# Retention's rotation moved from TensorE and ScalarE to VectorE, and a second token group multiplied before the norm's root

## The chip, the cores and the metric

The program runs on one core of one Trainium2 chip. The metric is the device time of one execution in microseconds. The engines are TensorE (PE, with its weight loads PEld), VectorE (DVE), ScalarE (ACT), GpSimd (POOL) and SyncE (SP), which issues the DMAs here.

## What is computed

Two blocks of two layers each act on a stream x of 512 tokens by 1024 channels in float32. The change lies in the first block only:

```
for l in range(2):
    h = rms_norm(x, norm_g[l])
    (gu, gv, gz, rq, rk, rv, rz, dq, dk, dv, dz, a_f, b_f, a_b, b_b) = split(h @ w_in[l])
    y_a = gmlp_branch(gu, gv, gz, ...)      # gelu(u) * mix(layer_norm(gelu(v))) * silu(z)
    y_b = retention_branch(rq, rk, rv, rz, ...)
    y_c = gdn_branch(dq, dk, dv, dz, ...)
    x = x + sum_n(sigmoid(h @ w_gate_n) * (y_n @ w_branch_out_n)) @ w_out[l]
x = rms_norm(x, final_norm_g)

def rotary(x):                              # on rq and rk, per head of 128
    x1, x2 = x[..., :64], x[..., 64:]
    return concatenate([x1 * cos - x2 * sin, x2 * cos + x1 * sin])

# retention, per head: o = (q k^T / sqrt(128) * mask) v, then a group norm;
mask = exp(where(rel >= 0, lf * rel, -lb * rel))      # lf, lb = log_sigmoid(decay_logit)
```

The second block is an attention with a SwiGLU, twice, and is the same in both kernels.

## The kernel before

**Data.** x is held as eight tiles of 128 channels by 512 tokens (`xT[:, k]`). Every projection is made to float32 precision from rounded halves: a weight granule of 512 KB comes by DMA into `raw[g % 4]` (`hi` waits for it), ACT casts it to `wh` (`hi(g)`, 128x1024), POOL writes `wl = raw - wh` in two pieces of 128x512 (`split`, L2361), and then PE does three matmuls for every 128-deep step: `wh*hh`, `wl*hh` and `wh*hl` (`three`, L830 to L832), where `hh` and `hl` are the rounded activations and their rest. There are four slots of each, and a slot's next load waits until its `wl` is written. A granule serves one `feature_tile` (eight steps, 24 matmuls of 128x512, one bank, a result with channels on the partitions) or a quarter of a `token_tiles` group (two steps for each of four banks, a result with tokens on the partitions).

**Order by hand.** Each engine has its own program, tied by semaphores. In a layer of the first block PE goes: token group of granules 0 to 3 (v of the gMLP), the small tile `wab`, feature tiles 4 to 7 (u), token group 8 to 11 (retention's v, `rv`), feature tiles 12 to 19 (retention's q and k), the retention products, feature tiles 20 to 35, and the rest. The four banks 0 to 3 are used in turn; `taken(i)` waits until the bank's last content is read out (`proj_taken`).

**The norm.** The first token group does not wait for the root of the norm: ACT writes `hh = x * g` (`gained_x`, L1702) and the squares (L1705), DVE writes `hl` (L2605) and adds the squares up (`ssum`, L2599), and the root is applied when ACT reads the banks out with Gelu (`vg`, L1775). In between, PE sums the squares per token (`norm_sums`, L840, after bank 1 of granule 1) and spreads the inverse root over a bank (`norm_row`, L847, after granule 1); from then on DVE writes x times the root (`ht`), ACT its `hh` (`normal_hi`) and POOL its `hl` (L2400) over the old ones, tile by tile as granules 0 to 3 are done.

**Retention.** ACT copies each q or k tile from its bank to `qraw` (L1806). PE multiplies `qraw` by a 128x128 matrix that swaps the halves with a sign (`rotate`, L968, into banks 4 to 7), DVE multiplies that by sin (L2705), `qraw` by cos (L2706) and adds (L2709). `mask_arg` makes the exponent of the mask on 128x896 in three DVE instructions (L2696 to L2698), ACT takes its exponential. `scores(h)` (L987) are four matmuls of 128x512 in float32, DVE multiplies them by the mask (`pb`, L2716), and PE makes the output from sixteen small ones (L998).

Of the kernel before, what the change touches and what calls it, by code (L numbers as in the profile page):

```python
# [16 lines left out]
F32 = mybir.dt.float32  # L17
# [5 lines left out]
P = 128  # L23
# [29 lines left out]
for _name, _n in (("ident", 128), ("ones", 128), ("rot", 128), ("cos", 512), ("sin", 512), ("dist", 896),  # L53
                  ("tri", 256), ("neg", 256), ("level", 2 * LEVELS * 128), ("own", 4), ("turn", 4)):
    CON[_name] = slice(_at, _at + _n)
    _at += _n
# [3 lines left out]
def constants():  # L60
# [5 lines left out]
    rot = np.zeros((P, P), np.float32)  # L66
    rot[i[:64] + 64, i[:64]] = -1.0
    rot[i[:64], i[:64] + 64] = 1.0
    c[:, CON["rot"]] = rot
# [3 lines left out]
    c[:, CON["sin"]] = np.tile(np.sin(ang), (2, 1))  # L73
# [55 lines left out]
def layer_signals(nc):  # L129
# [5 lines left out]
        rot_done=8, rot_taken=8, rope_ready=8,  # L135
        arg_ready=4, mask_ready=4, score_done=16, p_ready=16, o_done=4, o_taken=4,
# [17 lines left out]
DVE_OWN = 78 + 2 * (SUB - 1)  # L154
# [302 lines left out]
def build(nc, stream, params, consts, consts2, gains, xin, memin, out, n_granules):  # L457
# [226 lines left out]
    eye_loaded = nc.alloc_semaphore("eye_loaded")  # L684
    stored = nc.alloc_semaphore("stored")
# [7 lines left out]
    seventh_tile = nc.alloc_semaphore("seventh_tile")  # L693
# [46 lines left out]
    with block:  # L740
        @block.sync
        def _(sp):
# [20 lines left out]
            def projection_loads(a0, from_turn):  # L763

                with sp.Fori(a0 + from_turn, a0 + 5) as a:
# [60 lines left out]
        def _(pe):  # L826
# [23 lines left out]
            with pe.Fori(0, DEPTH) as L:  # L850
# [39 lines left out]
                def norm_sums():  # L890

                    pe.wait_ge(eye_loaded, 16)
# [10 lines left out]
                def token_tiles(g0, between={}):  # L903

                    for j in range(4):
                        weights(g0 + j)
                        for t in range(NT):
                            if j == 0:
                                taken(g0 + t)
                            if j == 0 and g0 == 0:  # L910
                                wait("x_ready", 5 + t)
                            for kk in range(2):
                                k = 2 * j + kk
                                if g0 == 0 and t == 0:
                                    wait("xl_ready", k + 1)
                                w = (g0 + j) % SLOTS
                                cols = slice(kk * T, (kk + 1) * T)
                                m = three(bk[t], hh[:, k, t * P:(t + 1) * P], hl[:, k, t * P:(t + 1) * P],
# [2553 lines left out]
```

## Time and profile before

| | |
|---|---|
| three runs | 2660.8, 2663.35, 2666.52 us (median 2663.35) |
| the profiled execution | 2666.1 us, its span on the core 2664.3 us |
| PE busy | 2590.4 us, 97% of the span |
| DVE, ACT, POOL busy | 39%, 42%, 50% |
| DMA | 215.08 MB, mean 81 GB/s |

The span runs from the first to the last instruction; the 1.8 us around it are in the execution's time only. PE is busy nearly throughout, so two things can change the time: work that PE no longer does, and moments in which it stands still or runs at the lower of its two clocks. The rows below are taken from those moments and from that work.

### The profile page before, as it was taken

To read this page: it belongs to the slowest core of one execution; us is meant where nothing else is said; L and a number is where in the kernel's file an instruction comes from. 1 tells how busy PE (TensorE), PEld (TensorE's weight loads), DVE (VectorE), ACT (ScalarE), POOL (GpSimd) and SP (SyncE) were. 2 spreads that over 40 slices of the span, in tenths; PEclk is the share of its full clock that TensorE was granted. 3 is DMA by queue.
4 is the path that set the end of the run, shared out by engine and by line. 5 is a ranking of instruction groups with operands and counts; after the bars stand their busy time and mean duration, and the time that the engine had idled before them with its cause. 6 is when DMAs were issued, how large, how long until landed. Compare 5 with 4: busy or idle time off the path is not lost.

```text
span 2664.3 us, 37275 instructions
## 1 busy us (share of the span) xinstructions
PE 2590.4 (97%) x13040; PEld 2080.5 (78%) x13040; DVE 1030.9 (39%) x2175; ACT 1117.2 (42%) x1708; POOL 1331.9 (50%) x1024
## 2 busy tenths in 40 slices
PE   7999999999999999999999999999999989999999
PEld 6778888888877788888886558888887756888887
DVE  4565542114466744212557553111005484311100
ACT  5428444325524645333546533333224464333321
POOL 5423664557542465556753114666547302456653
PEclk9999999999999999999999999999999999999999
DMA  4212112333231211332521012322333201233232
GB/s 178 87 46 74 56 33 65 101 95 121 81 94 40 80 33 33 95 94 75 162 82 56 22 32 79 110 94 94 102 111 103 80 16 48 88 101 94 94 103 71
DMA packets 62348, 215.08 MB, mean 81 GB/s; under 512 B 7296, under 2 KB 10496, under 8 KB 61824
## 3 DMA queue, kind: packets, MB, share of 16 engines
q1 hardware_dynamic: 62208, 213.28, 25.4%
q8 instruction: 80, 1.31, 0.2%
q14 instruction: 60, 0.49, 0.1%
HBM read 211.16 MB, written 2.10 MB: 80 GB/s over the span
## 4 chain that ended last, share of the span: by engine, by line
PE 59%; DVE 5%; ACT 1%; issue 1%; POOL 0%; DVEq 0%; ACTq 0%
PE bank L830 15%; PE bank L832 15%; PE bank L831 15%; PE pair L1588 2%; PE pair L830 1%; PE pair L831 1%; PE pair L832 1%; PE bank L1547 1%; PE bank L1548 1%; PE bank L1570 1%; PE pair L1401 1%; DVE soft L3255 1%; DVE pair L2796 0%; PE bank L1203 0%; DVE prod L2795 0%
## 5 line engine op out<-in xcount | busy, mean ns | idle before, releaser
L2361 POOL TENSOR_TENSOR wl<-raw,wh 128x512 fp32r<-128x512 f32 x768 | 1025.0, 1358 | 1174.2 <-ACT wh L1992 381.6
L830 PE MATMUL bank<-hh,wh 128*128 128x512 f32 x1584 | 627.5, 396 | 3.8 <-DVE y L2839 2.3
L832 PE MATMUL bank<-hh,wl 128*128 128x512 f32 x1584 | 617.2, 390 | 0.3 <-issue 0.3
L831 PE MATMUL bank<-hl,wh 128*128 128x512 f32 x1584 | 616.7, 389 | 0.0
L830 PEld LDWEIGHTS bank<-hh,wh 128*128 128x128 f32 x1584 | 297.4, 188 | 69.7 <-issue 6.4
L831 PEld LDWEIGHTS bank<-hl,wh 128*128 128x128 f32 x1584 | 297.5, 188 | 62.7 <-issue 2.9
L832 PEld LDWEIGHTS bank<-hh,wl 128*128 128x128 f32 x1584 | 297.3, 188 | 62.5
L2312 ACT CAST wh<-raw 128x1024 fp32r<-128x1024 f32 x120 | 125.5, 1048 | 254.0 <-PE pair L832 140.2
L830 PE MATMUL bank<-wh,hh 128*128 128x512 f32 (+2 forms) x352 | 140.7, 400 | 13.6 <-POOL wl L2361 12.4
L1992 ACT CAST wh<-raw 128x1024 fp32r<-128x1024 f32 x84 | 86.9, 1048 | 127.3 <-PE bank L832 107.8
L832 PE MATMUL bank<-wh,hl 128*128 128x512 f32 (+2 forms) x352 | 135.4, 385 | 0.0
L831 PE MATMUL bank<-wl,hh 128*128 128x512 f32 (+2 forms) x352 | 135.4, 385 | 0.0
L2924 DVE TENSOR_TENSOR gs<-gs,bank 128x512 f32<-128x512 f32 x24 | 16.4, 683 | 286.4 <-PE bank L832 286.4
L1746 ACT CAST wh<-raw 128x1024 fp32r<-128x1024 f32 x104 | 108.9, 1049 | 42.9 <-DMA raw<-stream 20.6
L1945 ACT CAST wh<-raw 128x1024 fp32r<-128x1024 f32 x72 | 75.3, 1046 | 85.5 <-PE pair L832 43.8
L3298 DVE TENSOR_TENSOR at<-row,bank 128x512 f32<-128x512 f32 x44 | 30.3, 688 | 202.2 <-PE bank L832 199.4
L831 PE MATMUL bank<-al,wh 128*128 (+1 forms) x264 | 102.7, 389 | 0.0
L830 PE MATMUL bank<-ah,wh 128*128 (+1 forms) x264 | 102.7, 389 | 0.0
L832 PE MATMUL bank<-ah,wl 128*128 (+1 forms) x264 | 102.7, 389 | 0.0
L1961 ACT ACTIVATE gs<-bank 128x512 f32<-128x512 f32 x48 | 28.8, 599 | 166.6 <-PE bank L832 166.5
L3295 DVE TENSOR_TENSOR at<-row,bank 128x512 f32<-128x512 f32 x44 | 30.3, 688 | 162.7 <-PE bank L832 162.1
L830 PEld LDWEIGHTS bank<-wh,hh 128*128 128x128 f32 x352 | 68.1, 194 | 25.9 <-issue 14.4
(461 smaller groups left out, 4833.0 us busy)
## 6 DMA issues: line engine op xcount, KB each, us to landing
raw<-stream SPq DMA_DIRECT2D x384, 512.0 KB, 3.5
mraw<-memin SPq DMA_DIRECT2D x3, 1024.0 KB, 6.5
par<-params SPq DMA_DIRECT2D x2, 1124.5 KB, 9.1
out<-xT SPq DMA_DIRECT2D x8, 256.0 KB, 2.0
con<-consts SPq DMA_DIRECT2D x1, 1540.0 KB, 15.5
xT<-xin SPq DMA_DIRECT2D x1, 1536.0 KB, 8.3
xT<-xin SPq DMA_DIRECT2D x1, 512.0 KB, 3.8
con<-consts SPq DMA_DIRECT2D x1, 512.0 KB, 3.1
```

What stands on the lines that cost most here:

```text
L830: mm(o, ah, bh, start=start, stop=False)
L831: mm(o, ah, bl, start=False, stop=False)
L832: return mm(o, al, bh, start=False, stop=stop)
L1588: x = mm(bk[value_bank(i, phase, a)], vv, pts[a % 2][kb][:, :], start=(kb == 0), stop=(kb == nk - 1))
L1746: nc.scalar.copy(wh[g % SLOTS][:, :], raw[g % SLOTS][:, :]).then_inc(hi_ready, 1)
L1945: nc.scalar.copy(wh[g % SLOTS][:, :], raw[g % SLOTS][:, :]).then_inc(hi_ready, 1)
L1961: A(gs[e][:, :], bk[e], ACT.Sigmoid).then_inc(s["gate_taken"].sem, 1)
L1992: nc.scalar.copy(wh[g % SLOTS][:, :], raw[g % SLOTS][:, :]).then_inc(hi_ready, 1)
L2312: nc.scalar.copy(wh[slot][:, :], raw[slot][:, :]).then_inc(hi_ready, 1)
L2361: m = TT(wl[slot][:, c], raw[slot][:, c], wh[slot][:, c].bitcast(F32), ALU.subtract)
L3295: V.tensor_tensor(at_[j][:, :], row[:, :], bk[2 * j], ALU.mult).then_inc(t["f_gate"].sem, 1)
L3298: V.tensor_tensor(at_[j][:, :], row[:, :], bk[2 * j + 1], ALU.mult).then_inc(t["f_up"].sem, 1)
```

## The change

In the first block, in both layers:

- **Rotation.** The matrix, `qraw` and ACT's copy are gone. DVE reads the projection's bank itself: two multiplications by sin on 64 partitions each, which write the other half of the partitions (the sign is in the table), one by cos on all, and the add. The bank is free when the cos product is done, so DVE now raises `proj_taken`. `scores(0)` stands before feature tile 19 instead of behind it, and its mask products behind the seventh rotation.
- **Masks.** ACT writes one side of the exponent (`back_arg`, 128x896), DVE the rest in one instruction in place of three.
- **Token groups.** `rv` follows v at once, as granules 4 to 7, with x that is not yet divided by the root; ACT applies the root when it reads it out. u follows as 8 to 11. The sums go to granule 2, bank 2, the spread root into the first granule of the second group. ACT's roots of the layer norm and DVE's layer norm come earlier.

At the program's start:

- x comes in three DMAs (tiles 0 and 1, 2 and 3, 4 to 7) around the first two granules; a small ACT instruction stands ahead of the wait for x, so that the table load does too; the first granule is cast and split in halves, PE begins when the first half is there and goes through the four banks with the first step before the second; the squares come behind the casts.

```diff
@@ sync: the start @@
-            sp.dma_start(xT[:, 2:KD], x_in[:, 2:KD]).then_inc(x_loaded[1], 16)
+            sp.dma_start(xT[:, 2:4], x_in[:, 2:4]).then_inc(x_loaded[1], 16)
             sp.dma_start(raw[1][:, :], stream[1]).then_inc(loaded[1], 16)
+            sp.dma_start(xT[:, 4:KD], x_in[:, 4:KD]).then_inc(eye_loaded, 16)
@@ tensor @@
-                token_tiles(0, {(1, 1): norm_sums, (1, 3): norm_row})
+                token_tiles(0, {(2, 2): norm_sums})
+                token_tiles(4, {(0, 1): norm_row})
...
-                token_tiles(8)
...
                 for i in range(8):
+                    if i == 7:
+                        scores(0)
                     feature_tile(12 + i)
...
-                    if i:
-                        rotate(i - 1)
-                rotate(7)
-                scores(0)
@@ scalar: the start @@
+            act.wait_ge(s["x_ready"].sem, 8)
+            A(root[:, 0, 4:5], eps_b[:, 0:1], ACT.Square)
             act.wait_ge(par_loaded, 16)
-            for k in range(KD):
-                if k in (0, 2):
-                    act.wait_ge(x_loaded[k // 2], 16)
-                gained_x(0, k, first_g)
-                if k % 2:
-                    act.wait_ge(loaded[k // 2], 16)
-                    nc.scalar.copy(wh[k // 2][:, :], raw[k // 2][:, :]).then_inc(hi_ready, 1)
+            for q in range(SLOTS):
...
+                for k in (2 * q, 2 * q + 1):
+                    A(hh[:, k], xT[:, k], ACT.Copy, scale=first_g[:, k:k + 1]).then_inc(first_hi, 1)
+                act.wait_ge(loaded[q], 16)
+                if q == 0:
+                    nc.scalar.copy(wh[0][:, 0:T], raw[0][:, 0:T]).then_inc(first_hi, 1)
+                    nc.scalar.copy(wh[0][:, T:], raw[0][:, T:]).then_inc(hi_ready, 1)
+                else:
+                    nc.scalar.copy(wh[q][:, :], raw[q][:, :]).then_inc(hi_ready, 1)
+                for k in (2 * q, 2 * q + 1):
+                    if k >= 4:
+                        act.wait_ge(s["sq_added"].sem, max(1, k - 4))
+                    A(sq2[k % 4][:, :], xT[:, k], ACT.Square).then_inc(s["sq_ready"].sem, 1)
@@ scalar: the second group's read-out, and the masks @@
+                for t in range(NT):
+                    inc(A(rv[t][:, :], bk[t], ACT.Copy, scale=root[:, 0, t:t + 1]), "proj_taken")
...
-                    inc(A(qraw[i % 4][:, :], bk[g % 4], ACT.Copy), "proj_taken")
...
+                    inc(A(mtmp[:, :], C["dist"], ACT.Copy, scale=lgt[:, 0, 4 + h:5 + h]), "back_ready")
@@ gpsimd @@
+            pool.wait_ge(first_hi, 3)
+            TT(wl[0][:, 0:T], raw[0][:, 0:T], wh[0][:, 0:T].bitcast(F32), ALU.subtract).then_inc(part_done, 1)
...
                     inc(TT(hl[:, k], ht[k % 4][:, :], hh[:, k].bitcast(F32), ALU.subtract), "hl_ready")
-                    if k == 3:
-                        lo(4)
+                    if k in (1, 3, 5):
+                        lo(8 + k // 2)
@@ vector @@
-                    step(V.tensor_scalar(m, C["dist"], 0.0, lgt[:, 3, h:h + 1], ALU.max, ALU.mult))
-                    step(V.tensor_scalar(mtmp[:, :], C["dist"], 0.0, lgt[:, 0, 4 + h:5 + h], ALU.min, ALU.mult))
-                    inc(V.tensor_tensor(m, m, mtmp[:, :], ALU.add), "arg_ready")
+                    inc(V.scalar_tensor_tensor(mask[h % 2][:, :], C["dist"], lgt[:, 3, h:h + 1], mtmp[:, :], ALU.mult, ALU.min),
+                        "arg_ready")
...
+                for i in range(8):
+                    dve.wait_ge(granule_done, L * G_LAYER + 13 + i)
+                    b = bk[i % 4]
+                    for low in (0, P // 2):
+                        to, of = slice(low, low + P // 2), slice(P // 2 - low, P - low)
+                        V.tensor_tensor(rt2[to, :], b[of, :], C["sin"][of, :], ALU.mult)
+                    V.tensor_tensor(rt1[:, :], b, C["cos"], ALU.mult).then_inc(s["proj_taken"].sem, 1)
+                    wait("proj_taken", 13 + i)
+                    dst = rqT[i][:, :] if i < 4 else rkT[i - 4]
+                    inc(V.tensor_tensor(dst, rt1[:, :], rt2[:, :], ALU.add), "rope_ready")
+                    if i in (2, 4):
+                        mask_arg(i // 2 - 1)
+                    if i == 6:
+                        scaled_scores(0)
```

On PE, at the program's first matmuls, there stands before (`lo_ready` is the whole first granule):

```order
L854 ISA [waits lo_ready]
L854 REGISTER_ALU [waits x_ready]
L830 MATMUL bank0<-wh0_56,hh_50 128x512 [waits xl_ready]
L831 MATMUL bank0<-wl0_60,hh_50 128x512
L832 MATMUL bank0<-wh0_56,hl_51 128x512
L854 REGISTER_ALU
L830 MATMUL bank0<-wh0_56,hh_50 128x512 [waits xl_ready]
```

and now (`part_done` is its first half):

```order
L858 ISA [waits part_done]
L858 REGISTER_ALU [waits x_ready]
L834 MATMUL bank0<-wh0_56,hh_50 128x512 [waits xl_ready]
L835 MATMUL bank0<-wl0_60,hh_50 128x512
L836 MATMUL bank0<-wh0_56,hl_51 128x512
L858 REGISTER_ALU
L834 MATMUL bank1<-wh0_56,hh_50 128x512 [waits x_ready]
```

The wait for the whole granule has moved behind twelve matmuls, three on each bank.

On PE, behind the last q and k tile (19) there stands before, up to the second head's scores:

```order
L968 MATMUL pair<-qraw_113,con 128x512 [waits rot_taken,proj_taken]
L854 REGISTER_ALU
L968 MATMUL pair<-qraw_114,con 128x512 [waits rot_taken,proj_taken]
L987 MATMUL bank<-rqT_101,y 128x512 [waits rot_taken,rope_ready]
L987 MATMUL bank<-rqT_101,y 128x512 [waits rot_taken]
L987 MATMUL pair<-rqT_101,y 128x512 [waits rot_taken] x2
```

and now, between tiles 18 and 19:

```order
L836 MATMUL bank<-hh,wl_62 128x512
L976 MATMUL bank<-rqT_101,y 128x512 [waits rope_ready]
L976 MATMUL bank<-rqT_101,y 128x512
L976 MATMUL pair<-rqT_101,y 128x512 x2
L864 REGISTER_ALU
```

The eight rotations are gone from PE, and the first scores no longer follow the last rotation.

On DVE, one rotation of a q tile before:

```order
L2705 TENSOR_TENSOR rt_118<-bank,con 128x512 [waits rot_done,rope_ready]
L119 REGISTER_ALU
L2706 TENSOR_TENSOR rt_105<-qraw_112,con 128x512 [waits dve_own]
L2709 TENSOR_TENSOR rqT_102<-rt_105,rt_118 128x512 [waits rot_taken]
L2705 TENSOR_TENSOR rt_118<-pair,con 128x512 [waits rot_done,rope_ready]
```

and now:

```order
L2741 TENSOR_TENSOR rt_118<-bank,con 64x512 [waits granule_done]
L2741 TENSOR_TENSOR rt_118<-bank,con 64x512
L2742 TENSOR_TENSOR rt_105<-bank,con 128x512
L2643 REGISTER_ALU
L2745 TENSOR_TENSOR rqT_102<-rt_105,rt_118 128x512 [waits proj_taken]
```

It is one instruction longer, waits for the granule in place of PE's rotation, and the multiplication by cos reads the bank.

## Rows read from the trace of the kernel before

**Rows 1.** The page, part 1: busy time of each engine.

```profile
PE 2590.4 (97%) x13040; PEld 2080.5 (78%) x13040; DVE 1030.9 (39%) x2175; ACT 1117.2 (42%) x1708; POOL 1331.9 (50%) x1024
```

**Rows 2.** Waits of PE: us in total, times, longest.

```profile
PE bank L830 <- POOL wl L2361: 16.0, 2, 12.4
...
PE pair L987 <- DVE rt L2706: 2.8, 2, 1.4
...
PE bank L830 <- ACT rv L1765: 1.4, 2, 0.7
...
PE bank L987 <- DVE pb L2716: 1.0, 2, 0.5
```

**Rows 3.** Timeline of the start: start us, duration us, engine, line, operation.

```profile
5.03 1.28 ACT L1702 ACT_TABLE_LOAD   x1 [5.03 <-DMA xT<-xin]
...
6.32 0.72 ACT L1702 ACTIVATE hh<-xT,first_g 128x512 fp32r<-128x512 f32 x1
...
8.60 1.03 ACT L1726 CAST wh<-raw 128x1024 fp32r<-128x1024 f32 x1
...
9.71 2.49 POOL L2361 TENSOR_TENSOR wl<-raw,wh 128x512 fp32r<-128x512 f32 x2 [9.26 <-ACT wh L1726]
10.46 0.72 ACT L1702 ACTIVATE hh<-xT,first_g 128x512 fp32r<-128x512 f32 x1 [0.83 <-DMA xT<-xin]
...
12.44 0.79 PE L830 MATMUL bank<-wh,hh 128*128 128x512 f32 x1 [12.44 <-POOL wl L2361]
...
13.27 0.74 DVE L2605 SCALAR_TENSOR_TENSOR hl<-xT,first_g,hh 128x512 fp32r<-128x512 f32 x1
...
16.32 0.40 PE L830 MATMUL bank<-wh,hh 128*128 128x512 f32 x1
```

**Rows 4.** Timeline of PE, 22 to 34 us: around the token sums.

```profile
22.22 0.39 PE L832 MATMUL bank<-wh,hl 128*128 128x512 f32 x1
...
26.10 1.63 PE L840 MATMUL pair<-con,ssum 128*128 128x1 f32 x8 [3.49 <-DVE ssum L2599]
...
29.30 0.77 PE L830 MATMUL bank<-wh,hh 128*128 128x512 f32 x1
...
33.27 0.39 PE L830 MATMUL bank<-wh,hh 128*128 128x512 f32 x1
```

**Rows 5.** Timeline of PE, the same sums in the second layer.

```profile
670.55 0.95 PE L840 MATMUL pair<-con,ssum 128*128 128x1 f32 x8
...
671.35 1.03 PE L840 MATMUL pair<-con,sq 128*128 128x1 f32 x8
```

**Rows 6.** Timeline of PE, two rotations with one feature tile between them.

```profile
117.65 1.02 PE L968 MATMUL bank<-qraw,con 128*128 128x512 f32 x2
124.00 1.02 PE L968 MATMUL pair<-qraw,con 128*128 128x512 f32 x2
```

**Rows 7.** Timeline of DVE: masks, and one rotation.

```profile
116.11 0.69 DVE L2696 TENSOR_SCALAR mask<-con,lgt 128x896 f32<-128x896 f32 x1
...
120.12 2.06 DVE L2698 TENSOR_TENSOR mask<-mask,mtmp 128x896 f32<-128x896 f32 x1
...
137.82 0.69 DVE L2705 TENSOR_TENSOR rt<-bank,con 128x512 f32<-128x512 f32 x1 [3.23 <-PE bank L968]
138.55 0.69 DVE L2706 TENSOR_TENSOR rt<-qraw,con 128x512 f32<-128x512 f32 x1
139.34 1.59 DVE L2709 TENSOR_TENSOR y<-rt,rt 128x512 f32<-128x512 f32 x1
```

**Rows 8.** Groups by line, forms apart: busy us, mean ns, idle before.

```profile
L2852 DVE TENSOR_SCALAR Y<-bank 64x256 f32<-64x256 f32 x16 | 6.8, 422 | 17.9 <-PE bank L1143 17.8
```

**Rows 9.** Timelines of ACT, POOL and PE at the end of the first group.

```profile
48.56 2.85 ACT L1775 ACTIVATE vg<-bank,root 128x512 f32<-128x512 f32 x4
...
48.78 1.30 POOL L2400 TENSOR_TENSOR hl<-ht,hh 128x512 fp32r<-128x512 f32 x1 [0.16 <-POOL hl L2400]
...
50.22 0.42 PE L830 MATMUL bank<-hh,wab_h 128*128 128x512 f32 x1
```

More of the change, by code:

```diff
@@ L52 @@
 _at = 0
-for _name, _n in (("ident", 128), ("ones", 128), ("rot", 128), ("cos", 512), ("sin", 512), ("dist", 896),
+for _name, _n in (("ident", 128), ("ones", 128), ("spare", 128), ("cos", 512), ("sin", 512), ("dist", 896),
                   ("tri", 256), ("neg", 256), ("level", 2 * LEVELS * 128), ("own", 4), ("turn", 4)):
@@ L905, in token_tiles @@
                     for j in range(4):
-                        weights(g0 + j)
-                        for t in range(NT):
-                            if j == 0:
-                                taken(g0 + t)
[L910 to L918, printed above, removed]
-                                          wh[w][:, cols], wl[w][:, cols], k == 0, k == KD - 1)
-                            if t == NT - 1:
+                        if (g0, j) == (0, 0):
+                            pe.wait_ge(part_done, 1)
+                        else:
+                            weights(g0 + j)
@@ new lines, in token_tiles @@
+                        order = [(kk, t) for kk in range(2) for t in range(NT)] if j == 0 else [(kk, t) for t in range(NT) for kk in range(2)]
+                        for kk, t in order:
+                            k = 2 * j + kk
+                            if j == 0 and kk == 0:
+                                taken(g0 + t)
+                                if g0 == 0:
+                                    wait("x_ready", 5 + t)
+                            if g0 == 0 and t == 0:
+                                if (j, kk) == (0, 1):
+                                    weights(0)
+                                wait("xl_ready", k + 1)
+                            w = (g0 + j) % SLOTS
+                            cols = slice(kk * T, (kk + 1) * T)
+                            m = three(bk[t], hh[:, k, t * P:(t + 1) * P], hl[:, k, t * P:(t + 1) * P],
+                                      wh[w][:, cols], wl[w][:, cols], k == 0, k == KD - 1)
+                            if (j, t) in between and kk == 1:
+                                between[j, t]()
+                            if (kk, t) == (1, NT - 1):
@@ L2393, in lo @@
                     split(g % SLOTS).then_inc(lo_ready, 1)
+                for g in range(4, 7):
+                    lo(g)
                 wait("wab_hi", 1)
@@ L2641, in _ @@
                                                ALU.mult, ALU.mult), "ht_ready")
+                    if k in (3, 5):
+                        layer_norm(k // 2 - 1)
+                for t in range(2, NT):
+                    layer_norm(t)
                 dl = R["decay"]
```

178 lines of the change are left out of this document (88 added, 90 removed).

## The prediction

> **What bounds the kernel now.** I read the page's busy times first: PE is busy for 97% of the span [rows 1], no other engine for more than half. So PE's own work sets the time, and only what PE stops doing, and where it stands still or runs slowly, can be won. Second, the waits of PE: one of 12.4 us at the very start for the first low part of the weights, two of 1.4 us in retention for DVE's rotation, two of 0.5 for its mask products, two of 0.7 for ACT's read-out of rv [rows 2]. Third, the timelines of those places. They show a cost that the waits do not: a 128x512 matmul follows the last every 0.43 us in the first microseconds (9 between 12.44 and 16.32) and every 0.227 afterwards (26 steps from 16.32 to 22.22) [rows 3, 4]; that is PE at the lower and the higher of its two clocks. After the stall before the token sums the nine from 29.30 to 33.27 are slow again [rows 4].
>
> **Program start.** Before, the table load begins only when x is there, at 5.03, and `hh` at 6.32; the cast of the first granule ends at 9.63, POOL's two pieces at 12.20, PE starts at 12.44 [rows 3]. Now the load stands ahead of the wait: `hh` from 5.05, the second about 0.63 later. The half cast then waits for the granule. Its arrival is not in a row; 2048 KB came between 5.03 and 10.46, in the order of issue, so 512 KB take 1.36 us and it is there at 6.4. Half of 1.03 us of cast with its overhead ends at 7.0, half of POOL's 2.49 at 8.35, and PE's 0.24 us behind it gives 8.6: 3.85 us won. Bounds: 1.3 (the table load alone) and 4.2. The sum does not hang on the following: the Trainium skill (ScalarE: Activation LUTs, What ACT_TABLE_LOAD costs) puts a switch at 2.66 us, with a drain behind the load; here the load took 1.28 and `hh` followed 0.01 later. By the page the earlier load would free 1.4 us more, but the first cast would still wait for its granule at 6.4.
>
> **Token sums of the first layer.** From 12.44 to 33.27, 20.83 us, PE did 45 matmuls and the sums [rows 3, 4]. Without the stall and with the clock kept it would be 9 slow ones (3.88), 36 at 0.227 (8.2) and the sums at the second layer's price, 1.85 us for both halves and 0.1 to go on [rows 5]: 14.0, so 6.8 are won. The condition is that DVE has the squares added when PE comes by. PE is there after nine slow and 57 fast matmuls, 8.6 + 3.9 + 12.9 = 25.4. DVE needed from 13.27 to about 26.05 for the last ten of its fourteen instructions there, 1.28 us each [rows 3, 4]. Now it has the first two tiles' `hl` by 7.2 and the next two tiles of x arrive at 7.8 in place of 10.5, and if those ten begin at 10.8, they end at 23.6. Slack 1.8 us. The low parts of granules 1 to 3 I get at 14, 17.7 and 21.2 (ACT's cast 1 us behind the data, POOL up to 3.4 us), needed at 15.9, 21.4 and 28.8. The bounds of this term are 1 and 7.
>
> In the second layer nothing stood still at the sums, so nothing is won.
>
> **Rotation off PE.** From one rotation to the next with a tile between is 6.35 us [rows 6]; the tile's 24 matmuls are 5.45 at 0.227; a rotation costs 0.90. Sixteen of them: 14.5 us. All of it is on PE's path. ACT's sixteen copies lie beside it and are worth nothing.
>
> **Waits in retention.** The two of 1.4 and the two of 0.5 come from the chain rotation on PE, rotation on DVE, scores, mask products behind the last tile. With `scores(0)` before tile 19 and needing only the fifth rotation, that tile hides it: 3.8 us. What is late next is DVE. A rotation there took 137.82 to 140.93, 3.11 us, with its add at 1.59; now a product more, 0.73: 3.84 us against a tile of 5.45 [rows 7]. That the half ones cost as much as a whole one I take from 422 ns for 64x256 elements [rows 8], which grows to 0.69 at 512. DVE was free for it at 116.1 [rows 7], some 8.8 us after the token mix began, since the masks no longer stand ahead; the bank of the first rotation is wanted 14.4 after it. Two masks (1.1 to 2.1 each) and four mask products (3.3) come between, so DVE runs nearly full from there: 7 x 3.84 + 3 + 3.3 = 33 us in the 31.4 until tile 19 is done. It comes out 1 to 2 us late at the eighth rotation. The second and third heads' scores still find their products ready, within 0.2 us, because PE has 7 us of its own work first. Bounds of this term: 0 and 4.
>
> The Trainium skill (VectorE: DVE Perf Modes, Two Vector instructions with no wait between them) says that an instruction whose operands start in another quarter of the partitions than the last is held until the earlier ones are finished, so the halves could not overlap. By it a step is the 0.73 that rows with a wait between them show (137.82 to 138.55), without it at best 0.69: 0.1 us per rotation, hidden either way.
>
> **Masks.** One DVE instruction for three and one on ACT, which idles there. Nothing on PE's path.
>
> **Second token group on x.** The new order of the tiles adds no work to PE. The wait for ACT's read-out changes its place: rv's (0.7 twice) is now covered by the `wab` tile, while v's Gelu, covered before, is exposed. Four Gelus took 2.85, 0.71 each, against three matmuls of 0.68 between two banks [rows 9]: 0.9 instead of 0.7 per layer, a loss of 0.4, at most 1.5. The `wab` tile needs the last low part: POOL ended it at 50.08 and PE wanted it at 50.22 [rows 9]. Now a granule's split stands before the last two; it starts about 2.3 us after the seventh granule is done and lasts up to 3.4, so it is over about when the eighth is done and the two casts come, and I find 1.3 us to spare. Sums, root and spread are the same instructions. SP's queue has the same loads in the same number; what is loaded differs only in its address.
>
> **Sum.** 3.85 + 6.8 + 14.5 + 3.8 - 0.4 = 28.6 us. Against the profiled execution's 2666.1 this gives 2637.5; that run is 2.75 above the median of the three, so for a median I forecast 2663.35 - 28.6 = 2634.8 us.
>
> **Rivals.**
>
> *The start is won, but the sums still stall.* DVE's instructions there last 0.7 or 1.77, by what POOL does; if nearly all take 1.77, ten last 17.7 us and the sums come at 28.5, 3 us late, and the clock falls with it. For it: most of the ten did overlap POOL. Against: 12.8 us measured for the same ten. The term of 6.8 shrinks to about 1: 2641 us. Chance 0.15.
>
> *The start is worth the table load only,* because the granule comes later than 6.4 or ACT's chain is longer: 2637.5. Chance 0.1.
>
> *DVE is behind in retention.* With 1 us more per rotation (4.8) the eighth ends 7 us later, and PE, which waits for mask products, loses about 6 per layer: 2635 + 12 = 2647. For it: nearly no slack by my count. Chance 0.12.
>
> *Slower than before: DVE becomes the bound of the eight q and k tiles.* If an operation that reads one half of the partitions and writes the other, and the cos product from the bank, ran at the price of contended ones (1.59, as the add in rows 7), a rotation would be 6.4 us, above the tile's 5.45; PE would wait for banks and for products. What PE loses per layer is about eight times the excess over 3.9: 20 us, twice 40, so 2675. It decides from 5.7 us per rotation, where 16 x 1.8 eats the whole gain. Against: a product from a bank was 0.69 each time [rows 7], also beside POOL. Chance 0.04.
>
> *The change does what it says, as summed.* Chance 0.59.
>
> **How the numbers follow.** The likeliest is 2634.8. Its own range is 2630 to 2639 (the runs before spread by 3 us each way, the terms by 2). To leave out no more than 2 in 10 the range must hold the two rivals at the start and the near half of the third: 2629 to 2645. Less than 0.2% (5.3 us, about what a measurement of this kernel can tell from no change) apart would need nearly all terms to fail: 0.03. Slower 0.04, faster 0.93.
>
> **What would show it.** The first matmul at 8.6 us; the lower clock only once, for nine matmuls; no wait for `ssum`; no rows of the rotation on PE, and PE's busy time down by about the 14.5 us; waits at the scores under 0.5 us in all; a wait of about 0.9 us for `vg` at granule 4 in each layer; DVE's half products at 0.69. The forecast is wrong if a half product takes 1.4 or more, if PE waits for DVE in tiles 16 to 19, or if a second slow stretch follows the sums.

## The result

The changed kernel takes 2640.9 us (median of 4 runs, 2637.4 to 2642.2) beside 2664.9 for the kernel before (4 runs, 2660.8 to 2666.7): a ratio of 0.9911, 95% interval 0.9899 to 0.9924. A later set of runs gave 2638.9 and 0.9902 (0.9886 to 0.9919). So 24 to 25 us were won of 28.6 forecast. The time lies inside the range, 6 us above the forecast value; the profiled span fell by 25.3 us, from 2664.3 to 2639.0.

PE's busy time on the page of the changed kernel, against [rows 1]:

```profile
PE 2574.6 (98%) x13008; PEld 2073.9 (79%) x13008; DVE 1033.4 (39%) x2175; ACT 1117.4 (42%) x1702; POOL 1330.9 (50%) x1024
```

That is 32 matmul records fewer, two for each of the sixteen rotations, and 15.8 us less of PE. Its waits, which answer to [rows 2] (total in us, times, longest):

```profile
PE bank L834 <- POOL wl L2376: 8.5, 1, 8.5
PE bank L1119 <- DVE LT L2905: 5.6, 4, 1.9
PE bank L834 <- POOL wl L2372: 3.6, 1, 3.6
...
PE bank L834 <- POOL hl L2418: 2.0, 4, 0.7
...
PE bank L834 <- ACT vg L1774: 1.6, 2, 0.8
```

The four waits in retention, for `rt` and for `pb`, are gone, and so are the two for `rv`. The one for `vg`, twice, was forecast. The one for `hl`, four times, is new and was not.

The start, against [rows 3], and the token sums, against [rows 4]: start us, duration us, engine, line, operation.

```profile
6.25 0.62 ACT L1728 CAST wh<-raw 128x512 fp32r<-128x512 f32 x1
...
6.95 1.33 POOL L2376 TENSOR_TENSOR wl<-raw,wh 128x512 fp32r<-128x512 f32 x1 [6.50 <-ACT wh L1728]
...
8.53 0.79 PE L834 MATMUL bank<-wh,hh 128*128 128x512 f32 x1 [8.53 <-POOL wl L2376]
...
25.57 0.95 PE L844 MATMUL pair<-con,ssum 128*128 128x1 f32 x8
26.38 1.03 PE L844 MATMUL pair<-con,sq 128*128 128x1 f32 x8
27.27 0.49 PE L834 MATMUL bank<-wh,hh 128*128 128x512 f32 x1
```

The cast begins at 6.25 and PE at 8.53. The sums come at 25.57 with no wait and take 1.7 us, and the matmuls behind them keep the higher clock.

**Where the 25.3 us lie.** Two marks are in both traces: the first matmul of the token mix, and the end of retention's last output. They divide the span.

| stretch | before | after | won | forecast |
|---|---|---|---|---|
| start to token mix, layer 1 | 107.32 | 98.42 | 8.90 | 10.45 |
| retention, layer 1 | 74.49 | 64.43 | 10.06 | 9.15 |
| then to the token mix of layer 2 | 566.60 | 570.11 | -3.51 | -0.2 |
| retention, layer 2 | 74.48 | 64.42 | 10.06 | 9.15 |
| the rest | 1841.4 | 1841.6 | -0.2 | 0 |

Retention gave more than forecast, the way to each token mix less. The rest of this document is about those two.

### The profile page after: what moved, and what is told of

The parts are those of the page before. It is cut to its first block, busy times and chain, and to the rows that moved or that the text cites. A ratio compares the mean times of both kernels' runs of the same rounds, so it can differ in the third digit from the quotient of the medians.

```text
span 2639.0 us, 37066 instructions
## 1 busy us (share of the span) xinstructions
PE 2574.6 (98%) x13008; PEld 2073.9 (79%) x13008; DVE 1033.4 (39%) x2175; ACT 1117.4 (42%) x1702; POOL 1330.9 (50%) x1024
## 4 chain that ended last, share of the span: by engine, by line
PE 60%; DVE 5%; ACT 1%; issue 1%; POOL 0%; DVEq 0%; ACTq 0%
PE bank L834 15%; PE bank L836 15%; PE bank L835 15%; PE pair L1585 2%; PE pair L834 1%; PE pair L835 1%; PE pair L836 1%; PE bank L1544 1%; PE bank L1545 1%; PE bank L1567 1%; PE pair L1398 1%; DVE soft L3289 1%; DVE pair L2830 0%; PE bank L1199 0%; DVE prod L2829 0%
## 5 line engine op out<-in xcount | busy, mean ns | idle before, releaser
L834 PEld LDWEIGHTS bank<-wh,hh 128*128 128x128 f32 x352 | 67.6, 192 | 25.1 <-issue 10.5
```

What stands on the lines that cost most here:

```text
L834: mm(o, ah, bh, start=start, stop=False)
```

## What the new trace shows of the loss

PE in the `wab` tile, which takes one part of `hl` per three matmuls, and POOL ahead of it:

```profile
61.63 0.39 PE L836 MATMUL bank<-hh,wab_l 128*128 128x512 f32 x1
62.30 0.50 PE L834 MATMUL bank<-hh,wab_h 128*128 128x512 f32 x1 [0.28 <-POOL hl L2418]
62.63 0.39 PE L835 MATMUL bank<-hl,wab_h 128*128 128x512 f32 x1
62.86 0.39 PE L836 MATMUL bank<-hh,wab_l 128*128 128x512 f32 x1
63.98 0.50 PE L834 MATMUL bank<-hh,wab_h 128*128 128x512 f32 x1 [0.73 <-POOL hl L2418]
```

```profile
42.36 1.30 POOL L2418 TENSOR_TENSOR hl<-ht,hh 128x512 fp32r<-128x512 f32 x1 [1.41 <-ACT hh L1763]
...
45.33 3.25 POOL L2372 TENSOR_TENSOR wl<-raw,wh 128x512 fp32r<-128x512 f32 x2 [0.16 <-POOL hl L2418]
48.53 1.30 POOL L2418 TENSOR_TENSOR hl<-ht,hh 128x512 fp32r<-128x512 f32 x1
...
57.56 3.25 POOL L2372 TENSOR_TENSOR wl<-raw,wh 128x512 fp32r<-128x512 f32 x2 [0.16 <-POOL hl L2418]
60.78 1.47 POOL L2418 TENSOR_TENSOR hl<-ht,hh 128x512 fp32r<-128x512 f32 x1
62.41 1.52 POOL L2418 TENSOR_TENSOR hl<-ht,hh 128x512 fp32r<-128x512 f32 x1 [0.16 <-POOL hl L2418]
```

From 42.36 on POOL goes from one instruction to the next, with gaps of 0.16 us at most. One round of two low parts of h and one split takes from 42.36 to 48.53, 6.17 us, where PE needs 5.45 for a granule. Three rounds put POOL 2.2 us behind. The wait rows say 0.28 and 0.73; the distances from one matmul to the next are 0.67 and 1.12 in place of 0.23, so the layer loses 0.44 + 0.89 = 1.33 us, and with the slightly slower matmuls behind each stop about 1.5. For these two stops the wait row leaves out 0.16 us each, and about 0.25 with the matmuls behind them.

Behind the first layer's retention there is a second thing. Both kernels have the same stall, 1.88 us for `LT`, a tile that DVE makes at the head of the gated part (`gdn_branch`). Granted clock in windows of 2 us around it: the window, its length, busy time of each engine with instruction counts, PE's clock, DMA share, GB/s; after first, then before.

```profile
284.00:286.00 2.00, 1.25 (x33) 1.16 (x34) 1.17 (x5) 0.26 (x1) 1.52 (x2) 0.94 0.00 0
286.00:288.00 2.00, 2.00 (x6) 1.32 (x4) 0.00 (x0) 1.06 (x2) 0.14 (x1) 0.50 0.00 0
288.00:290.00 2.00, 2.00 (x50) 1.66 (x50) 0.07 (x1) 0.00 (x0) 0.00 (x0) 0.71 0.00 0
```

```profile
302.00:304.00 2.00, 0.54 (x25) 0.54 (x27) 1.80 (x6) 0.26 (x1) 1.45 (x3) 1.00 0.00 0
304.00:306.00 2.00, 2.00 (x27) 1.42 (x22) 0.00 (x0) 1.33 (x2) 0.85 (x1) 1.00 0.00 0
```

The stall is as long in both, yet the clock halves behind it in one and not in the other. Half the length of all stretches of low clock behind the start, which is the full-clock time that they can cost, comes to about 12 us in each of the two kernels. The stretch behind the sums, forecast to go, went (3.4 us), and so did one at 1436; new ones came at 286, 920 and 2136.

## Experiments

All ratios are to the kernel before on the same chip in the same set of runs. Where a whole-kernel ratio is too coarse (its interval is 4 us each way) the verdict rests on the stretches named above. That of retention repeats well: the nine traces in which it is the same work as in the changed kernel, its own among them, gave 64.42 or 64.43 us in both layers. The way from there to the next token mix repeats less well, since stretches of low clock fall into it, and one wait that the profile puts down to nothing (at 645 us) was 0.4 to 1.3 us long; there the text goes by the distance between the same matmuls in two traces.

### 1. The last split behind the last two low parts of h

```diff
                     wait("hh_ready", k + 1)
...
-                    if k in (1, 3, 5):
+                    if k in (1, 3):
                         lo(8 + k // 2)
-                for g in range(11, 36):
+                for g in range(10, 36):
```

> The changed kernel, with POOL's split of the eleventh granule behind the last two low parts of the normalised activations (hl) and not before them. Theory A (the order on POOL makes the low parts late): in the changed kernel PE waited 1.0 us per layer for hl in the wab tile, which with its restarts cost 1.5 us; both waits go in both layers, 3 us less, about 2638 us against 2641. Theory B (VectorE's contention slows POOL, whatever the order): the last two low parts come later by the slowed rounds before them; a wait of 0.3 to 0.7 us per layer stays and the gain is under 1.5 us. If the order of POOL does not matter at all: 2641.

Measured: 2634.9 us, ratio 0.9903 (0.9886 to 0.9919), span 2632.0. POOL now waits for ACT ahead of the last two, and no row of PE's waits names `hl`:

```profile
58.34 1.30 POOL L2418 TENSOR_TENSOR hl<-ht,hh 128x512 fp32r<-128x512 f32 x1 [1.15 <-ACT hh L1763]
59.79 1.29 POOL L2418 TENSOR_TENSOR hl<-ht,hh 128x512 fp32r<-128x512 f32 x1 [0.16 <-POOL hl L2418]
61.25 5.76 POOL L2372 TENSOR_TENSOR wl<-raw,wh 128x512 fp32r<-128x512 f32 x4 [0.16 <-POOL hl L2418]
```

From PE's first matmul to the token mix it is 87.8 us, against 89.9 and 90.4 in the two traces of the changed kernel. Of these 2.1 to 2.6 us, 0.6 to 1.2 are three to six slow matmuls fewer at the very start; 1.4 to 1.5 are left. In the second layer the stretch to the token mix is hardly shorter (569.86 for 570.11), because this run had a stretch of low clock at 182 us that cost 1.6; from just ahead of the first stop for `hl` to just behind the second, PE gains 1.4 us there too. So the order on POOL is enough to bring the wait about or to remove it, and 1.5 us a layer is its price. The span is 7 us shorter: 3 of them are this, and most of the rest is clock, of which this run lost 6.8 us and the changed kernel 12.0.

### 2. The layer norm on DVE behind the projections

DVE's four `layer_norm` calls move from between the `ht` products to behind the logarithm's arguments, so that POOL's splits run alone.

> The changed kernel, with VectorE's four layer norm steps of v back behind the gate arithmetic, where the kernel before had them, and POOL's order unchanged. Theory B (contention): POOL's splits in the second token group fall from 3.25 us to about 2.55, a round of two low parts and a split from 6.1 to 5.45 or less, and the waits for hl go: 3 us less, about 2638. Theory A (order alone): the splits may be shorter but the low parts still stand behind a split that begins only with its cast; waits of 0.5 us or more per layer stay, 2640 to 2641.

Measured: 2651.1 us, ratio 0.9961 (0.9947 to 0.9975), span 2647.6: slower than the changed kernel. POOL did get faster, and the `hl` wait is gone:

```profile
41.83 1.30 POOL L2418 TENSOR_TENSOR hl<-ht,hh 128x512 fp32r<-128x512 f32 x1 [1.39 <-ACT hh L1763]
...
44.75 2.54 POOL L2372 TENSOR_TENSOR wl<-raw,wh 128x512 fp32r<-128x512 f32 x2 [0.16 <-POOL hl L2418]
47.25 1.29 POOL L2418 TENSOR_TENSOR hl<-ht,hh 128x512 fp32r<-128x512 f32 x1
```

A round is 5.42 us in place of 6.17, just under PE's 5.45. The whole excess of the round is thus DVE's: POOL's split takes 3.25 beside the layer norm and 2.54 alone, while DVE's products there take 1.66 in place of 0.69. The changed kernel needs both for its wait, the early split and the slowed rounds; experiment 1 takes away the one, this one the other, and the wait goes either way. The Trainium skill (GPSIMD Engine Reference, Specifications) says that POOL shares its SBUF interfaces with DVE's instructions that have two SBUF inputs. The trace agrees, and shows that both pay; a product that reads a PSUM bank took 0.69 beside POOL too.

But the decays wait for the layer norm now, and PE for them:

```profile
94.49 1.03 PE L956 MATMUL pair<-gdec,con 128*128 128x16 f32 x4 [3.92 <-DVE gdec L2696]
95.37 0.77 PE L834 MATMUL bank<-hh,wh 128*128 128x512 f32 x1
95.94 0.63 PE L835 MATMUL bank<-hl,wh 128*128 128x512 f32 x1
```

These are 3.9 us of stall and twelve matmuls at the lower clock (0.43 in place of 0.23), in each layer, which neither theory had. First matmul to token mix is 94.7 us, 4.8 more than in the changed kernel, and the way to the second layer's token mix 577.3, 7.2 more, of which a further stretch of low clock at 189 us is nearly 2. So the early place of the layer norm, with its 1.5 us a layer, is the cheaper one of the two.

### 3. The token sums a granule earlier

```diff
-                token_tiles(0, {(2, 2): norm_sums})
+                token_tiles(0, {(1, 1): norm_sums})
```

> The changed kernel, with the token sums back behind bank 1 of the second granule. My account of the start: PE asks for them at about 18.6 us, VectorE has the squares added at 23.4, so PE stands still for 4.9 us, and the lower clock comes back: the sums take 3.2 us in place of 1.85 and about nine matmuls 0.43 us in place of 0.227. Together 8 us more, about 2649 us. Rival: the clock stays up behind the stall, then it is 5 us more, 2646.

Measured: 2648.6 us, ratio 0.9953 (0.9936 to 0.9969), span 2645.2.

```profile
19.46 0.39 PE L836 MATMUL bank<-wh,hl 128*128 128x512 f32 x1
23.51 1.05 PE L844 MATMUL pair<-con,ssum 128*128 128x1 f32 x8 [3.65 <-DVE ssum L2617]
24.42 1.44 PE L844 MATMUL pair<-con,sq 128*128 128x1 f32 x8
25.72 0.77 PE L834 MATMUL bank<-wh,hh 128*128 128x512 f32 x1
26.29 0.63 PE L835 MATMUL bank<-wl,hh 128*128 128x512 f32 x1
```

The stall comes back, the sums take 2.2 us in place of 1.7, and the 13 matmuls from 25.72 on are slow, 0.2 us more each. The token mix comes at 106.45 in place of 98.42: 8.0 us, of which 1.0 is five more slow matmuls at the very start (they also bring PE later to the sums, so that the stall is shorter than the 4.9 expected) and 7 the sums' place; 3.65 stand in the wait row. So the place is worth what was forecast (6.8), and this stall cost twice its row. In the changed kernel DVE ended its sum at 23.4, PE asked at 25.57: 2.2 us to spare where 1.8 were forecast.

### 4. Split and read-out together

Experiment 1, and ACT's first three Gelu read-outs of v released bank by bank, where all four waited for the whole granule.

> As e1_split_last, and ACT's Gelu of v may read each of the banks 0 to 2 as soon as its own last matmul is done and not only at the granule's end. The 0.8 us wait per layer for the first Gelu goes (0.9 us with the restart): 1.8 us less than e1_split_last, about 2636. Rival: the Gelus start before the inverse root or the table load is there, or the next wait follows at bank 3; then within 0.5 us of e1_split_last.

Measured: 2634.9 us, ratio 0.9895 (0.9879 to 0.9912), span 2633.6. Neither the `hl` nor the `vg` wait is left, and in place of the gap to 35.16 PE runs on at 34.99. First matmul to token mix is 87.7 us. Against experiment 1's 87.8 the `vg` wait does not show, since 12 matmuls were slow at this run's start and 6 at that one's; six are 1.2 us. From matmul to matmul against the changed kernel it does: PE gains 0.9 us at the place of the wait in each layer, 1.15 with the matmuls behind it, and 1.5 at `hl`. The ratios of experiments 1 and 4 can't be told apart.

### 5. The changed kernel again

> The changed kernel itself once more, beside the runs that follow. Theory (the low-clock stretches that follow stalls fall by the program's own timing): the same ratio to the kernel before within 0.15%, 0.991, and in the trace the same stretches of low clock at 286, 921, 1304, 1380, 2004 and 2136 us, 12 us of lost clock in all. Rival (they fall by chance in each execution): other places, and a sum that differs by 3 us or more.

Measured: 2638.9 us, ratio 0.9902, span 2639.9. The stretches of low clock behind 286, 920, 1304, 1380, 2002 and 2136 us are there again; two more came, at 820 and 2639; that at 1304 was shorter. It is 12.5 us in all. The ratio is 0.0009 lower than at first, within the interval and within the expected 0.0015. So the places mostly belong to the program, but neither theory is whole: some come and go. In the other kernels, whose only difference is some microseconds upstream, the sum was between 5.1 (experiment 11) and 15.8 us (experiment 2). The slow matmuls at the very start were 9 and 12 in these two traces, and 6 to 14 in all. The Trainium skill (TensorE: Matmul & The Clock Gate, What's actually happening) says that this number differs from run to run of one kernel; the two traces agree.

### 6 and 7. One, and three, more products per rotation on DVE

```diff
+                    for x in range(1):
+                        V.tensor_tensor(qraw[1 + x][:, :], b, C["cos"], ALU.mult)
                     V.tensor_tensor(rt1[:, :], b, C["cos"], ALU.mult).then_inc(s["proj_taken"].sem, 1)
```

The second kernel has `range(3)`.

> Each of the sixteen rotations has one more 128x512 product from the bank on DVE, into a tile that nothing reads: 0.72 us more of DVE per rotation, 5.8 per layer. Theory (DVE stands 0.9 us ahead of the second head's scores, and waits 0.8 and 2.7 us for PE ahead of the last two rotations): 5.8 less 3.5 comes out behind the eighth rotation, 2.3 us; the first mask product of the second head comes at 146.5 where PE wants it at 145.1, so PE waits about 1.4 per layer, 1.8 with the restart: 3 to 4 us over the changed kernel. Rival A (DVE is far from the path in retention): within 1 us of the changed kernel. Rival B (DVE already sets the pace there): the whole 11.6 us more.

> Three more products per rotation: 2.16 us more, a rotation of about 5.5 to 6, 17.3 us of DVE per layer. Theory: less the 3.5 us of idle time, 13.8 comes out behind the eighth rotation, and less the 0.9 of slack 12.9 of it are lost per layer: 26 us over the changed kernel, slower than before. First waits of PE at the scores of the first head (about 6 us) or one tile ahead. Rival (each rotation hides behind a tile of 5.45 us, so only what exceeds it counts): 3 to 5 us per layer, 6 to 10 in all.

With one, 2640.3 us, ratio 0.9909 (0.9893 to 0.9926); with three, 2657.2, ratio 0.9979 (0.9969 to 0.9988). PE in retention, one more product, then three:

```profile
147.10 1.98 PE L976 MATMUL bank<-rqT,y 128*128 128x512 f32 x4 [0.72 <-DVE pb L2731]
```

```profile
134.95 3.78 PE L976 MATMUL bank<-rqT,y 128*128 128x512 f32 x4 [4.84 <-DVE y L2747]
138.52 2.79 PE L976 MATMUL pair<-rqT,y 128*128 128x512 f32 x4
...
155.62 1.98 PE L976 MATMUL bank<-rqT,y 128*128 128x512 f32 x4 [1.83 <-DVE pb L2731]
```

Retention took 65.43 us with one, 1.0 more than the changed kernel, and 74.3 and 76.0 with three, 10 and 11.6 more. The places are the expected ones, the scores of the first head and those of the third; the amounts are smaller (1.8 and 12.9 were expected), because a product more behind another costs 0.61 us in place of 0.72, 4.9 per layer, three cost 1.80 in place of 2.16, 14.4 per layer, and the third mask in the first of the two took 1.15 in place of 1.91. DVE's cover in the changed kernel is its 0.8 and 2.7 us of waiting and 0.9 of earliness, 4.4 in all or 0.55 us per rotation. 14.4 less 4.4 is the 10. 4.9 less 4.4 is 0.5, where 1.0 was measured: adds and masks change their length from kernel to kernel (the second mask took 2.06 us for 1.15), so the cover is known to about half a microsecond. Up to there more DVE work is free, beyond it all of it counts. The low clock that doubled the length of the first head's scores in the second block of rows (3.78 for x4) costs nothing more, since DVE is behind throughout. The rows of DVE in the changed kernel that show how little is left:

```profile
138.30 1.39 DVE L2741 TENSOR_TENSOR rt<-bank,con 64x512 f32<-64x512 f32 x2 [2.67 <-PE bank L836]
139.70 0.69 DVE L2742 TENSOR_TENSOR rt<-bank,con 128x512 f32<-128x512 f32 x1
140.43 0.82 DVE L2745 TENSOR_TENSOR y<-rt,rt 128x512 f32<-128x512 f32 x1
141.41 1.91 DVE L2722 SCALAR_TENSOR_TENSOR mask<-con,lgt,mtmp 128x896 f32<-128x896 f32 x1 [0.17 <-ACT mtmp L1809]
143.44 1.50 DVE L2731 SCALAR_TENSOR_TENSOR pb<-bank,mask 128x512 f32<-128x512 f32 x2
```

DVE waits 2.7 us for the last tile, and after its rotation and a mask the second head's first product is there at 144.2; PE wants it at 145.10.

### 8. The old masks

```diff
-                    wait("back_ready", h + 1)
-                    inc(V.scalar_tensor_tensor(mask[h % 2][:, :], C["dist"], lgt[:, 3, h:h + 1], mtmp[:, :], ...), "arg_ready")
+                    m = mask[h % 2][:, :]
+                    step(V.tensor_scalar(m, C["dist"], 0.0, lgt[:, 3, h:h + 1], ALU.max, ALU.mult))
+                    step(V.tensor_scalar(mtmp[:, :], C["dist"], 0.0, lgt[:, 0, 4 + h:5 + h], ALU.min, ALU.mult))
+                    inc(V.tensor_tensor(m, m, mtmp[:, :], ALU.add), "arg_ready")
@@ scalar @@
-                    inc(A(mtmp[:, :], C["dist"], ACT.Copy, scale=lgt[:, 0, 4 + h:5 + h]), "back_ready")
+                    inc(A(deviation[:, 0:8], lgt[:, 0, :], ACT.Copy), "back_ready")
```

> The changed kernel with the old exponent of the masks: three DVE instructions of 128x896 (0.69, 0.69, 1.33) in place of one (1.15 to 1.9), and ACT's 128x896 instruction shrunk to 128x8. What the masks' part of the change is worth alone. Prediction: nothing, within 1 us of the changed kernel. Theory from the trace of the changed kernel: the two masks between the rotations are hidden by DVE's 3.5 us of waits, the third stands between the eighth rotation and the second head's mask products, with 0.9 us to spare, and is 1 to 1.5 us longer: 0.1 to 1 us per layer, 0.2 to 2 in all. Rival (DVE full): 1.3 us for each of eight masks, 10 us.

Measured: 2639.2 us, ratio 0.9902 (0.9885 to 0.9918), so nothing by the whole kernel. The stretch says otherwise: 65.59 and 65.61 us, 1.16 more per layer.

```profile
146.88 1.98 PE L976 MATMUL bank<-rqT,y 128*128 128x512 f32 x4 [0.91 <-DVE pb L2732]
```

The masks' part of the change is worth 2.3 us, where the prediction had nothing.

### 9. A narrow rotation in the kernel before

```diff
-                    inc(mm(bk[4 + i % 4], C["rot"], qraw[i % 4][:, :], start=True, stop=True), "rot_done")
+                    inc(mm(bk[4 + i % 4][:, 0:16], C["rot"], qraw[i % 4][:, 0:16], start=True, stop=True), "rot_done")
```

> The kernel before, with each of the sixteen rotation matmuls on PE cut from 512 columns to 16; DVE still reads whole banks, so the rotated q and k are not the reference's. Nothing else is changed: what the rotation's work on PE is worth alone. Theory (the whole 0.90 us is on PE's path): a rotation of 16 columns leaves 0.1 us, 16 x 0.8 = 12.8 us less, the waits of 1.4 and 0.5 us stay: ratio 0.9952. Rival (PE would only wait longer for DVE there, since a rotation's chain sets the pace): 2 us or less.

This kernel leaves out 496 of the 512 columns of each rotation, so its result is not the reference's; only its time is of use.

Measured: 2657.6 us, ratio 0.9976 (0.9967 to 0.9986), half of what was expected. Two rotations with a tile between, against [rows 6], and the places of the waits behind the last one:

```profile
117.22 0.29 PE L968 MATMUL bank<-qraw,con 128*128 128x16 f32 x2
122.91 0.29 PE L968 MATMUL pair<-qraw,con 128*128 128x16 f32 x2
...
146.50 0.40 PE L968 MATMUL pair<-qraw,con 128*128 128x16 f32 x2 [0.56 <-ACT qraw L1806]
...
149.99 1.13 PE L987 MATMUL pair<-rqT,y 128*128 128x512 f32 x2 [0.42 <-DVE rt L2706]
152.48 1.98 PE L987 MATMUL bank<-rqT,y 128*128 128x512 f32 x4 [1.37 <-DVE pb L2716]
```

The pitch is 5.69: a rotation of 16 columns still costs 0.24 us beside the tile's 5.45, not 0.1. So 0.66 are saved by each, and 0.6 of that is lost again behind the last one, in a wait for ACT's copy. Retention fell from 74.49 to 69.81 us, 4.7 a layer, 9.4 in all; the profiled span fell by 12.6 (the clock again, 6.8 us lost in place of 11.9), the median only by 7.3. The wait for `rt` shrank by what that for `pb` grew. The rotation's work was on PE's path; narrower products don't take it off, leaving it out does: in the changed kernel the tiles begin at 107.45, 112.89, 118.33 and 123.77 us, 5.44 apart, 0.91 less than before.

### 10. The start

The changed kernel with the table load behind x again (the small ACT instruction left out), and with PE waiting for the whole first granule. Each ran once, so only the trace is read.

> The changed kernel without the small ACT instruction ahead of the wait for x, so that the table load stands behind x again. Theory (ACT's chain then ends behind the granule's arrival at 6.25 us): the first hh at 6.3, the first cast at 7.6 in place of 6.25, the first matmul at 9.9 in place of 8.5, 1.35 us later, and the span longer by as much. Rival (the granule's arrival sets the start): first matmul at 8.5 to 8.6, nothing lost. Second rival: the 1.35 us at the start comes back at the next waits, for vg and hl, and the span is the same.

> The changed kernel, but PE waits for both low halves of the first granule. Theory: the second ends at 9.5 us, so the first matmul is at 9.75, 1.2 us later, still nine slow ones, the token sums without a wait at 26.8, and the first group's end 1.2 us later. Rival (PE comes later at every wait that others set, so vg and hl take the loss up): the token mix starts at 98.4 as before.

First matmul at 9.84 and at 9.76 us, against 8.53: 1.3 and 1.2 later, as expected. The token mix came at 100.66 and 99.42, against 98.42: 2.2 and 1.0 later. Nothing was taken up by the waits for `vg` and `hl`, which stayed as they were (0.8 a layer, and 2.0 in all): the chains that end there are started by PE itself. The 0.9 beyond the 1.3 in the first are more slow matmuls (14 to 9 at the start). The spans, 2639.7 and 2638.9 beside 2639.0, show neither: these traces lost 8.5 and 10.5 us of clock, the changed kernel 12.0.

### 11. High parts first

Experiment 4, and at the start PE takes the four products of the high parts as soon as the first cast is there, ahead of its wait for POOL:

```diff
-                            pe.wait_ge(part_done, 1)
+                            pe.wait_ge(first_hi, 3)
...
+                        if (g0, j) == (0, 0):
+                            wait("xl_ready", 1)
+                            for t in range(NT):
+                                taken(t)
+                                wait("x_ready", 5 + t)
+                                mm(bk[t], hh[:, 0, t * P:(t + 1) * P], wh[0][:, 0:T], start=True, stop=False)
+                            pe.wait_ge(part_done, 1)
```

> An attempt to beat both kernels: the last split behind the last low part of h and v's read-outs bank by bank (both as in the run that joined them, 0.9895), and at the start PE takes the four products of the two high parts as soon as the first cast is there, ahead of the wait for POOL's low part. Theory: first matmul at 7.1 us in place of 8.7, four slow ones of 0.43 until 8.8, then the rest with no wait; everything up to the second granule is 1.4 us earlier, if its low part is there in time (14.2; wanted at 14.4): ratio 0.989. Rival (granule 1's low part comes too late, because PE is early and POOL not): the gain ends there, the ratio stays at 0.9895 within 0.0003. Rival on the clock: the slow matmuls are as many as before, so the gain is 1.4; were it a fixed time from the first one, it would be the same.

Measured: 2631.6 us (2627.4 to 2633.6), ratio 0.9878 (0.9861 to 0.9894), span 2627.9.

```profile
7.69 2.07 PE L920 MATMUL bank<-wh,hh 128*128 128x512 f32 x4 [7.69 <-ACT wh L1741]
9.56 0.63 PE L935 MATMUL bank<-wl,hh 128*128 128x512 f32 x1
```

The weights' cast came 0.6 us later than in the changed kernel here (it waited 0.37 us for the granule's DMA), so PE starts at 7.69 and not at 7.1; the second granule is no wait. The token mix is at 94.70, 1.8 earlier than in experiment 4 and 3.7 earlier than in the changed kernel. Of the 1.8, 1.1 are the earlier first matmul and 0.6 three slow matmuls fewer (9 for 12), and the rival with a late second granule did not come. By the ratios the kernel can't be told from experiment 4 (0.9895). It has the lowest median: 33.3 us under the kernel before in its set, of which 6 to 9 by the ratios go beyond the changed kernel. The stretches give 6.0 of them: 3.7 to the first token mix and 2.25 on the way to the second (567.86 for 570.11). The clock, of which this run lost 5.1 us for 12.0, has its part in what is beyond.

## Why the prediction was right, and where not

**Program start: right.** 3.85 us were forecast, 3.91 measured; the cast is at 6.25 (6.4 forecast), PE at 8.53 (8.6). One link was other than told: the cast follows the second `hh` with no wait, so ACT's own chain and not the granule's arrival sets it here; in experiment 11 the arrival did. Experiment 10 puts 1.3 us on the table load, the 1.28 of its row and no more, and 1.2 on the half granule.

**Token sums: right.** There is no wait, one slow stretch at the start with nine matmuls, and DVE is ready at 23.4 (23.6). Experiment 3 turns the stall back on, and its place costs 7.0.

**Rotation off PE: right.** It is 0.91 us per tile. Experiment 9 was a poor probe for it, and confirms it only after its own 0.24 is known.

**Waits in retention: right in kind, too small in size.** 7.25 us of rotation and 1.9 of waits were forecast per layer, 10.06 came. The term that was mis-sized is the waits. Their rows say 1.40 and 0.49; from matmul to matmul they cost 1.56 and 0.76 (2.42 and 1.62 where 0.86 is the undisturbed pair of two). With the restart behind the 0.18 wait at the first rotation that is 2.7, and 7.24 and 2.7 make 9.9 of the 10.06. Each of these waits cost more than its row says.

**Masks: wrong, small.** "Nothing on PE's path" holds only as long as DVE has room, and the same text had found it nearly full. Experiment 8 gives 2.3 us. It did no harm to the sum: the `pb` waits were counted as gone altogether, and with the old masks one of 0.9 a layer is back, so the masks belong to the term of the waits.

**DVE's room: the right picture, wrong numbers.** A rotation took 2.8 to 3.9 us (3.84 forecast), since the add met POOL only in some; so DVE was not 1 to 2 us late at the eighth but waited 2.7 for it, and the products for the second head have 0.9 to spare. Experiments 6 and 7 put the turning point at about 0.55 us more per rotation; the rival with 1 us more and 6 per layer did not come, and overstated its price (8 less 4.4 is 3.6). That the halves cost as much as a whole was right: the two together take 1.39 us and start 0.70 apart, where two whole products behind each other start 0.61 apart (experiment 6), so the halves do not overlap.

**The `vg` wait: right.** Its row is 0.78 us a layer, and experiment 4, which takes it away, gains 0.9 there and 1.15 with the matmuls behind it (0.9 forecast).

**The `hl` chain: wrong, and it is the step that failed in the sum.** "I find 1.3 us to spare" was found for one round: a split that begins 2.3 us after a granule and lasts up to 3.4 is done in time. What counts is the round: 6.17 us of POOL per 5.45 of PE, and the lag of the first two is carried into the third. Three rounds take 2.2 us, more than the spare. Nor was the DVE side counted, although the change itself moved the layer norm beside the splits. With the layer norm elsewhere the round is 5.42 and the lag does not build up (experiment 2); with the split elsewhere it does no harm (experiment 1). The price is 1.5 us a layer, 3.0 in all.

**The clock: not in the forecast.** The text treated the low clock as something that follows a stall and goes when it goes. It did go at the sums. But new stretches came behind a stall that both kernels have, at 286 and 920 us, which cost 1.4 and 1.3 us from matmul to matmul, and a third at 2136, so that the total stayed at 12. Why those and not others is open: no run here controls where they fall. They are large enough to hide a difference of 2 us between two kernels' medians.

The shortfall in the span, 28.6 less 25.3, is then: `hl` 3.0; the clock behind `LT` in the first layer 1.4; the turns (transposes) behind retention in the first layer 0.3 (PE waited 0.93 us for `y` in place of 0.57 and 1.21 for `qT` in place of 1.03, but part of it comes back before the next mark); the rest of the span 0.2; less 1.8 that retention gave beyond the forecast. That is 3.1 for 3.3. The 0.2 of the rest is itself a sum of larger things: the clock took 1.3 us at 920 and 1.5 at 2136 and gave back 2.1 at 1436, and a wait for `PT` behind 2136 was 0.6 us shorter. So the forecast value came as near as it did partly by luck: the wait in `hl` and the waits in retention were missed in opposite directions, and the clock's changes nearly cancel.

## What to carry to other kernels

When instructions of two producers alternate in one queue, compare the length of a whole round with the consumer's pitch, and multiply the difference by the number of rounds; that the first instruction is in time says nothing of a later one. Price a stall from matmul to matmul, not by the wait row, and add the slow matmuls behind it. To see whether a part of a change pays a microsecond or two, time a stretch between two marks that nothing else touches: retention repeated to 0.01 us here, where the runs of one kernel spread by 5.

## What was not expected of the hardware

- The same stall of 1.88 us, with the same work on both sides, is followed by six matmuls at 0.43 us in the changed kernel and by none in the kernel before.
- A matmul of 128x16 f32 costs 0.24 us of PE's path between tiles of 128x512, more than a quarter of the 0.90 that 512 columns cost (experiment 9).
- The price of POOL and DVE beside each other is on both (changed kernel against experiment 2): POOL's split 3.25 us for 2.54, DVE's product with two SBUF inputs 1.66 for 0.69, its scaling with one 0.90 for 0.55. Products that read a bank stay at 0.69.
